# Attention stage of a two-layer encoder: where a gated eviction, the last projection units and the softmax bound stand

## The chip, the cores and the metric

One NeuronCore of one Trainium2 chip runs the whole kernel in a single launch. The metric is the device time of one execution in microseconds; the median of several runs counts. The engines are TensorE (PE, with PEld for its weight loads), VectorE (DVE), ScalarE (ACT), GpSimd (POOL) and SyncE (SP, which here only issues the weight DMAs). Each engine runs its own list of instructions in order, and they meet through semaphores.

## The reference

Two post-norm layers over x of shape (1, 512, 1024). What matters here, per layer:

```python
proj = jnp.einsum("btd,de->bte", x, w_in)            # q/k/v of the delta rule, z, beta, decay, q/k/v of attention, gates
...                                                  # branch A: gated delta rule, 8 heads of 128, both directions
o_dn = (o_dn * lax.rsqrt(jnp.mean(o_dn * o_dn, axis=-1, keepdims=True) + RMS_EPS)
        * dn_norm_w * jax.nn.silu(z))
...                                                  # branch B: attention, 16 query heads, 4 key heads, |i - j| <= 128
p = jax.nn.softmax(jnp.concatenate([s, sink], axis=-1), axis=-1)[..., :-1]
o = jnp.einsum("bnhgqk,bnkhd->bnqhgd", p, vb)
gate_a, gate_b = jnp.split(jax.nn.sigmoid(gates), 2, axis=-1)
merged = gate_a * (o_dn @ w_branch_a) + gate_b * (o_sw @ w_branch_b)
x = layer_norm(DN_ALPHA * x + merged @ w_out, ...)
x = layer_norm(DN_ALPHA * x + swiglu_ffn(x, ...), ...)
```

The softmax of a query has one extra column, the head's sink logit, in its maximum and in its denominator.

## The kernel before

**Weights.** All weights arrive as units of 128 x 1024 f32 over one queue (SP, L437) into three slots. A slot is loaded again when TensorE has finished the unit in it. POOL splits each unit into a high part (L488) and a low part (L491); TensorE forms each product as high x high, high x low and low x high (L527, L528, L529). A unit of features has 8 steps of three 512-column matmuls into one PSUM bank.

**The delta-rule stage.** 24 q/k/v units come first. Then 8 heads run one after another (levels of a triangular inverse, then a scan of 4 steps). Between their dependent matmuls TensorE does fill work, taken from a fixed list: `FILL` is the order in which the 28 units of z, gate A and attention's q, k, v are streamed, and `ORDER` adds work without weights to it: ("o", i) turns head i's normed output with 4 transposes, ("t", i) turns a value tile. `SHARE` and `SHARE_LAST` say how many steps are done at which spot of a head; what is left after the last head is done behind the scores of attention's block 0 (`fill(len(STEPS) - filled[0])`). Entries alternate between PSUM banks 6 and 7; an entry starts only when the one two before it has been evicted (`fill_free`). ACT evicts z, g, q, k, v and t in `fill_out`; DVE evicts o and multiplies it by dn_norm and silu(z) (L1549), and forms the cosine part of q and k. At the end of `ORDER` stand v0, o0, z7, t0, o1, o2, g7, o3, o4, v1, o5, o6, t1, o7. In the last head ACT also scales the outputs of the earlier heads and takes silu of their z (`head_out`).

**Attention.** 16 blocks n (4 groups of heads g x 4 blocks of 128 queries b), each against 2 or 3 key blocks. Per block: TensorE scores (L887, masks L892) into banks 0 to 2; DVE takes the row maximum (`stats`, L1666), the bound with the sinks (L1669), its negative (L1671) and the sink term (L1672); ACT forms the exponentials with their sums (L1274) and that of the sink (L1277); DVE adds to the denominator and takes the reciprocal (L1694, L1696); TensorE turns the probabilities (L929) into banks 4 to 6; ACT copies the first of them (L1288), DVE the others (L1705); TensorE multiplies by the values (L943), DVE scales (L1711). Into each block TensorE also puts one unit, half before and half behind the value matmuls: `block_unit(n)`, in bank 3, for n < 8 a gate B unit, for n >= 8 one of W_A. It starts when unit n-1 has been evicted (`att_free`), by ACT for gate B and by DVE's `branch_a` (L1684) for W_A, with its gate multiplied in. In DVE's loop over n, `branch_a(n - 9)` stands behind the denominators and behind `stats(n + 1)`, ahead of the copies of pT.

What sets all orders is the program text; there is no planner. Merging, output projection, layer norms and the feed-forward follow and are not touched.

Of the kernel before, what the change touches and what calls it, by code (L numbers as in the profile page):

```python
# [17 lines left out]
F32 = mybir.dt.float32  # L18
# [8 lines left out]
P = 128  # L27
SEQ = 512
D = 1024
DEPTH = 2  # L30
# [51 lines left out]
for _h in range(0, HEADS, 2):  # L82
    _a, _b, _c = SIDE[_h // 2 * 3:_h // 2 * 3 + 3]
    FILL += [("z", _h), ("g", _h), _a, _b, ("z", _h + 1), ("g", _h + 1), _c]


ORDER = [(kind, n, f) for f, (kind, n) in enumerate(FILL)]
_at = {(kind, n): p for p, (kind, n, f) in enumerate(ORDER)}
ORDER = (ORDER[:_at["v", 0] + 1] + [("o", 0, None), ORDER[_at["z", 7]], ("t", 0, None), ("o", 1, None), ("o", 2, None),
       ORDER[_at["g", 7]], ("o", 3, None), ("o", 4, None), ORDER[_at["v", 1]], ("o", 5, None), ("o", 6, None),  # L90
       ("t", 1, None), ("o", 7, None)])
STEPS = [(p, k) for p, (kind, n, f) in enumerate(ORDER) for k in range(1 if f is None else KT)]


# [23 lines left out]
def trunk(nc, x_in, stream, w_ba, conv_w, a_log, dt_bias, dn_norm, sinks, ln_rows, ln_cols, consts, masks, trig_in, out):  # L118
    with ExitStack() as ctx:
# [39 lines left out]
        exp_a = place("exp_a", [P, DEPTH * 16], F32)  # L159
        dtb = place("dtb", [P, DEPTH * 16], F32)  # L160
        snk = place("snk", [P, DEPTH * 16], F32)
        tab = place("tab", [P, HEADS, 6, 2, CHUNKS], F32)
        rn = place("rn", [P, 2 * HEADS, CHUNKS], F32)
        rno = place("rno", [P, HEADS, CHUNKS], F32)
# [95 lines left out]
        def flat(ap):  # L260

            return ap.rearrange("p c t -> p (c t)")
# [251 lines left out]
        def _(pe):  # L514
# [109 lines left out]
            for l in range(0, DEPTH):  # L624
# [11 lines left out]

                feature_pair(l * PAIRS + AT_QKV, l * 16)

                pe.wait_ge(ready_bf, 7)
                pe.wait_ge(ba_split, l * 2 + 2)  # L640
                for k in range(KT):
                    ins = product(PS[0:32, 4, :], bah[:, k, :], bal[:, k, :], xh[:, k, :], xl[:, k, :],
# [339 lines left out]
        def _(act):  # L982
# [49 lines left out]
            for l in range(0, DEPTH):  # L1032
# [45 lines left out]
                def head_out(i):  # L1078

                    for c in range(CHUNKS):  # L1080
                        ins = A(o_dn[:, i, c, :], o_dn[:, i, c, :], ACT.Copy, scale=rno[:, i, c:c + 1])
                    ins.then_inc(on_ready, 1)
                    z = flat(raw[:, i, :, :])
                    A(z, z, ACT.Silu).then_inc(z_silu, 1)

# [93 lines left out]
                def head(h, s, more):  # L1179
                    n = l * HEADS + h  # L1180
                    for lev in range(1, 7):
                        for r in range(2):
                            act.wait_ge(vx_mm[r], n * 6 + lev)
                            if lev in BLOCK_LEVELS:
                                new = PS[:, 3 * r + 2, :].rearrange("p (c t) -> p c t", c=CHUNKS)
                                for a, b in new_blocks(lev, r == 1):
                                    ins = copy(X[r][a, :, b], new[a, :, b])
                                ins.then_inc(x_upd[r], 1)
                            else:
                                copy(X[r][:].rearrange("p c t -> p (c t)"), PS[:, 3 * r + 2, :]).then_inc(x_upd[r], 1)  # L1190
                        if lev % 2 == 0:
                            fill_out(ISSUED[h, f"L{lev}"])
                        if not more and lev == 1:
                            act.wait_ge(rno_dve, l * 4 + 1)
                            A(rno[:, 0:HEADS - 1, :], rno[:, 0:HEADS - 1, :], ACT.Sqrt).then_inc(rno_act, 1)
                        if not more and lev > 1:
                            act.wait_ge(rno_dve, l * 4 + 2)
                            head_out(lev - 2)
                    for r in range(2):
                        act.wait_ge(e_mm[r], n + 1)  # L1200
                        A(V[r][:].rearrange("p c t -> p (c t)"), PS[:, 3 * r, :], ACT.Copy,
                          scale=E_SCALE).then_inc(e_ready[r], 1)
                    if more:
                        front_turned(n + 1, 1 - s)
                        fill_out(ISSUED[h, "E"])
                    else:
                        head_out(5)
                    for step in range(CHUNKS):
                        chunk = (step, CHUNKS - 1 - step)
                        for r in range(2):  # L1210
# [17 lines left out]
                        if step == 1:  # L1228
# [2 lines left out]
                            fill_out(ISSUED[h, "S0"])  # L1231
                            if not more:
                                head_out(6)
                        if step == 2:
                            fill_out(ISSUED[h, "S1"])
                    fill_out(ISSUED[h, "S2"])
# [15 lines left out]

                act.wait_ge(rno_dve, l * 4 + 3)
                A(rno[:, HEADS - 1, :], rno[:, HEADS - 1, :], ACT.Sqrt).then_inc(rno_act, 1)
                fill_out(ORDER.index(("o", 5, None)))
                act.wait_ge(rno_dve, l * 4 + 4)
                head_out(HEADS - 1)
                fill_out(len(ORDER))

                def group_out(g):  # L1260
# [4 lines left out]
                for n in range(GROUPS * CHUNKS):  # L1265
                    g, b = divmod(n, CHUNKS)
                    m = l * GROUPS * CHUNKS + n
                    nb = min(b + 2, CHUNKS) - max(b - 1, 0)
                    act.wait_ge(stats_step, m * 4 + 3)
                    if n > 0:  # L1270
                        act.wait_ge(p_turned, m)
                        act.wait_ge(den_step, m * 2)
                    for q in range(GQ):
                        A(pr[:, q, 0:nb, :], PS[:, 0:nb, q * P:(q + 1) * P], ACT.Exp, bias=mn[:, q:q + 1],  # L1274
                          scale=ATT_SCALE, accum_out=den[:, q:q + 1]).then_inc(probs, 1)
                    act.wait_ge(stats_step, m * 4 + 4)
                    A(es[:], es[:], ACT.Exp).then_inc(sink_exp, 1)  # L1277
                    if b == 0 and g > 0:
                        group_out(g - 1)
                    if 1 <= n <= KT:  # L1280
# [66 lines left out]
        def _(dve):  # L1347
# [17 lines left out]
            for r in range(2):  # L1365
                TS(neg_bf[r][:], tri[r], 1.0, NEG_BIG, ALU.subtract, ALU.mult).then_inc(ready_bf, 1)
            nc.vector.memset(ln_rs[:], 0.0).then_inc(ready_bf, 1)
            for s in range(2):
                dve.sem_inc(ff_h, 1)
            dve.wait_ge(ready_bf, 7)  # L1370

            def output_gain(l, n, c):
                m = l * 2 + n
# [10 lines left out]
            for l in range(0, DEPTH):  # L1384
# [267 lines left out]
                head(HEADS - 1, 1, False)  # L1652
                dve.wait_ge(o_ss, (l + 1) * HEADS)
                TS(rno[:, HEADS - 1, :], rno[:, HEADS - 1, :], 1.0 / P, RMS_EPS, ALU.mult, ALU.add).then_inc(rno_dve, 1)
                fill_out(ORDER.index(("o", 3, None)))
                dve.wait_ge(rno_act, l * 2 + 2)
                nc.vector.reciprocal(rno[:, HEADS - 1, :], rno[:, HEADS - 1, :]).then_inc(rno_dve, 1)

                def stats(n):
# [5 lines left out]
                    dve.wait_ge(scores, m + 1)  # L1665
                    nc.vector.tensor_reduce(mx[:], PS[:, 0:hi - lo, :].rearrange("p j (q t) -> p q j t", q=GQ),  # L1666
                                            mybir.AxisListType.XY, ALU.max).then_inc(stats_step, 1)
                    dve.wait_ge(stats_step, m * 4 + 1)
                    STT(mx[:], mx[:], ATT_SCALE, sinks_of, ALU.mult, ALU.max).then_inc(stats_step, 1)  # L1669
                    dve.wait_ge(stats_step, m * 4 + 2)  # L1670
                    TS(mn[:], mx[:], -1.0, None, ALU.mult).then_inc(stats_step, 1)  # L1671
                    TT(es[:], sinks_of, mx[:], ALU.subtract).then_inc(stats_step, 1)  # L1672

                def group_out(g):
                    for t, bk in ((0, 2), (1, 6)):
# [12 lines left out]
                for n in range(GROUPS * CHUNKS):  # L1688
                    g, b = divmod(n, CHUNKS)
                    m = l * GROUPS * CHUNKS + n  # L1690
                    lo, hi = max(b - 1, 0), min(b + 2, CHUNKS)
                    dve.wait_ge(probs, m * 4 + 4)
                    dve.wait_ge(sink_exp, m + 1)
                    TT(den[:], den[:], es[:], ALU.add).then_inc(den_step, 1)  # L1694
# [3 lines left out]
                        group_out(g - 1)  # L1698
                    if b > 0 and n < GROUPS * CHUNKS - 1:
                        stats(n + 1)  # L1700
                    if n > KT:
                        branch_a(n - 1 - KT)
                    dve.wait_ge(p_turned, m + 1)
                    for j in range(1, hi - lo):
                        ins = nc.vector.tensor_copy(pT[:, j, :], PS[:, 4 + j, :])  # L1705
# [231 lines left out]
```

## Time and profile before

| | us |
|---|---|
| runs, median of 3 | 2601.8 (2597.61 to 2605.43) |
| profiled execution | 2598.42 |
| its span, first to last instruction | 2596.6 |
| PE busy | 2422.8 (93%) |
| DVE busy | 1145.5 (44%) |
| POOL busy | 1134.9 (44%) |
| ACT busy | 789.1 (30%) |
| attention of layer 0, about | 600 to 820 |
| attention of layer 1, about | 1890 to 2103 |

Busy times are of instructions that compute; waits aren't in them. A wait is shown in brackets behind the instruction that ended it, with what released it. Matmuls overlap, so that a 512-column matmul shows 0.39 us while the next starts 0.23 us later.

### The profile page before, as it was taken

To read this page: it belongs to the slowest core of one execution; us is meant where nothing else is said; L and a number is where in the kernel's file an instruction comes from. 1 tells how busy PE (TensorE), PEld (TensorE's weight loads), DVE (VectorE), ACT (ScalarE), POOL (GpSimd) and SP (SyncE) were. 2 spreads that over 40 slices of the span, in tenths; PEclk is the share of its full clock that TensorE was granted. 3 is DMA by queue.
4 is the path that set the end of the run, shared out by engine and by line. 5 is a ranking of instruction groups with operands and counts; after the bars stand their busy time and mean duration, and the time that the engine had idled before them with its cause. 6 is when DMAs were issued, how large, how long until landed. Compare 5 with 4: busy or idle time off the path is not lost.

```text
span 2596.6 us, 35628 instructions
## 1 busy us (share of the span) xinstructions
PE 2422.8 (93%) x14240; PEld 1998.1 (77%) x14240; DVE 1145.5 (44%) x2066; ACT 789.1 (30%) x2114; POOL 1134.9 (44%) x674
## 2 busy tenths in 40 slices
PE   8999999988988989999999999999889898999997
PEld 6877877777877778888778778778778777788885
DVE  4666677653333251110156666766533335411103
ACT  3644433453322021110045444434543221211100
POOL 4543232323323646666545432332332246566665
PEclk9999999999999999999999999999999999999999
DMA  3221111111112323333222111111111133233332
GB/s 129 90 66 42 38 50 44 40 38 41 41 33 98 106 73 97 98 98 97 91 98 82 58 49 38 46 41 38 46 41 41 33 106 113 74 97 97 114 94 85
DMA packets 53252, 181.69 MB, mean 70 GB/s; under 512 B 7392, under 2 KB 8032, under 8 KB 53088
## 3 DMA queue, kind: packets, MB, share of 16 engines
q1 hardware_dynamic: 44496, 160.71, 20.1%
q10 hardware_dynamic: 8592, 18.69, 2.3%
q8 instruction: 114, 1.87, 0.3%
q14 instruction: 50, 0.41, 0.1%
HBM read 169.94 MB, written 4.19 MB: 67 GB/s over the span
## 4 chain that ended last, share of the span: by engine, by line
PE 76%; DVE 13%; ACT 5%; issue 3%; DMA 1%; POOL 1%; ACTq 0%; DVEq 0%; SPq 0%; POOLq 0%
PE PS L527 20%; PE PS L528 19%; PE PS L529 19%; PE PS L887 3%; DVE Y L1599 3%; PE PS L943 2%; DMA w_raw<-stream 1%; PE PS L761 1%; PE PS L848 1%; ACT DT L1144 1%; DVE att L1666 1%; PE PS L705 1%; ACT pr L1274 1%; PE PS L772 1%; DVE V L1587 1%
## 5 line engine op out<-in xcount | busy, mean ns | idle before, releaser
L488 POOL TENSOR_SCALAR wh<-w_raw 128x1024 fp32r<-128x1024 f32 (+1 forms) x301 | 323.5, 1075 | 1350.6 <-DMA w_raw<-stream 1350.2
L491 POOL TENSOR_TENSOR wl<-w_raw,wh 128x1024 fp32r<-128x1024 f32 (+1 forms) x301 | 722.6, 2401 | 25.1
L527 PE MATMUL PS<-xh,wh 128*128 128x512 f32 x1664 | 689.4, 414 | 19.6 <-POOL wl L491 6.9
L529 PE MATMUL PS<-xl,wh 128*128 128x512 f32 x1664 | 658.3, 396 | 0.0
L528 PE MATMUL PS<-xh,wl 128*128 128x512 f32 x1664 | 657.0, 395 | 0.0
L527 PEld LDWEIGHTS PS<-xh,wh 128*128 128x128 f32 x1664 | 318.7, 192 | 79.1 <-POOL wl L491 8.2
L529 PEld LDWEIGHTS PS<-xl,wh 128*128 128x128 f32 x1664 | 317.4, 191 | 69.9
L528 PEld LDWEIGHTS PS<-xh,wl 128*128 128x128 f32 x1664 | 319.5, 192 | 55.2
L1500 DVE SCALAR_TENSOR_TENSOR conv_acc<-PS,cw,conv_acc 128x510 f32<-128x510 f32 x192 | 143.9, 749 | 120.5 <-ACT conv_acc L1113 115.3
L1848 DVE TENSOR_TENSOR hf<-sg,PS 128x512 f32<-128x512 f32 x44 | 30.2, 687 | 357.7 <-PE PS L529 357.7
L527 PE MATMUL PS<-wh,hh 128*128 128x512 f32 x352 | 138.9, 395 | 3.4 <-POOL wl L491 3.4
L528 PE MATMUL PS<-wh,hl 128*128 128x512 f32 x352 | 140.3, 398 | 0.0
L529 PE MATMUL PS<-wl,hh 128*128 128x512 f32 x352 | 138.1, 392 | 0.0
L1739 DVE SCALAR_TENSOR_TENSOR x<-x,PS 128x1024 f32<-128x1024 f32 x12 | 14.6, 1220 | 279.1 <-PE PS L529 279.1
L1587 DVE TENSOR_TENSOR V<-PS,lev_mask 128x512 f16<-128x512 f32 x192 | 123.5, 685 | 12.9 <-PE PS L761 10.1
L1190 ACT CAST X<-PS 128x512 f16<-128x512 f32 x128 | 73.7, 586 | 133.4 <-PE PS L780 123.6
L1666 DVE TENSOR_REDUCE att<-PS 128x4 f32<-128x1024 f32 (+1 forms) x32 | 47.7, 1489 | 130.1 <-PE PS L892 92.8
L1335 ACT ACTIVATE hh<-hf 128x512 fp32r<-128x512 f32 x44 | 27.8, 632 | 252.5 <-DVE hf L1848 252.5
L1599 DVE TENSOR_TENSOR Y<-PS,Y 128x512 f16<-128x512 f32 x128 | 85.4, 688 | 27.3 <-PE PS L772 27.2
L1320 ACT ACTIVATE ln_rs<-ln_rs 128x1 f32<-128x1 f32 x16 | 3.2, 203 | 293.4 <-DVE ln_rs L1762 293.4
L1274 ACT ACTIVATE pr<-PS,att 128x256 f32<-128x256 f32 (+1 forms) x128 | 65.9, 529 | 82.8 <-DVE att L1671 82.8
L772 PE MATMUL PS<-V,X 128*128 128x128 f16 x768 | 75.6, 221 | 15.0 <-DVE V L1587 5.8
(249 smaller groups left out, 4084.3 us busy)
## 6 DMA issues: line engine op xcount, KB each, us to landing
w_raw<-stream SPq DMA_DIRECT2D x300, 512.0 KB, 3.5
x<-x_in ACTq DMA_DIRECT2D x6, 512.0 KB, 7.2
qx<-qx ACTq DMA_DIRECT2D x48, 64.0 KB, 2.0
raw<-raw ACTq DMA_DIRECT2D x32, 64.0 KB, 2.1
ln_g<-ln_rows ACTq DMA_DIRECT2D x4, 512.0 KB, 4.3
ln_b<-ln_rows ACTq DMA_DIRECT2D x4, 512.0 KB, 5.8
x_park<-x ACTq DMA_DIRECT2D x4, 512.0 KB, 4.9
x<-x_park ACTq DMA_DIRECT2D x4, 512.0 KB, 6.6
```

Source lines behind the costliest of these rows:

```text
L488: nc.gpsimd.tensor_scalar(wh[s][:, w], w_raw[s][:, w], 1.0, 1.0, ALU.mult, ALU.mult).then_inc(w_hi_done, 1)
L491: nc.gpsimd.tensor_tensor(wl[s][:, w], w_raw[s][:, w], wh[s][:, w].bitcast(F32), ALU.subtract).then_inc(split_done, 1)
L527: mm(o, ah, bh, start=first, stop=False)
L528: mm(o, al, bh, start=False, stop=False)
L529: return mm(o, ah, bl, start=False, stop=last)
L772: ins = mm(PS[:, 3 * r + 1, c * P:(c + 1) * P], X[r][:, c, :], V[r][:, c, :], start=True, stop=True)
L887: ins = mm(PS[:, j, q * P:(q + 1) * P], qx[:, g // 2 * GQ + q, b * P:(b + 1) * P], kz[:, g, (lo + j) * P:(lo + j + 1) * P], start=q == 0, ...
L1190: copy(X[r][:].rearrange("p c t -> p (c t)"), PS[:, 3 * r + 2, :]).then_inc(x_upd[r], 1)
L1274: A(pr[:, q, 0:nb, :], PS[:, 0:nb, q * P:(q + 1) * P], ACT.Exp, bias=mn[:, q:q + 1], scale=ATT_SCALE, accum_out=den[:, q:q + 1]).then_inc( ...
L1500: STT(conv_acc[s][:, lo:hi], PS[:, s, lo + d:hi + d], w, conv_acc[s][:, lo:hi], ALU.mult, ALU.add).then_inc(conv_step, 1)
L1587: TT(V[r][:], bank(3 * r), rows(y_mask[r][lev]), ALU.mult).then_inc(v_ready[r], 1)
L1599: TT(Y[r][:], bank(3 * r + 1), Y[r][:], ALU.add).then_inc(y_upd[r], 1)
```

## The change

In the order of units, z7 and g7 come ahead of v0 and v1, and the tail of `ORDER` is o0, v0, o1, o2, t0, o3, o4, v1, o5, o6, t1, o7. Silu of z is taken apart from `head_out` (`z_out`), so that the last head's has been taken before the end of the scan. ACT's exponentials become a function, and those of block 0 are called ahead of the last evictions of the fill list; two intermediate `fill_out` calls (one on ACT, one on DVE) fall away. On DVE the bound is formed by one operation from the row maximum and a stored negative of the sinks, and `branch_a` moves to the front of its block.

```diff
+FILL[-7:] = [("z", 6), ("g", 6), ("q", 7), ("z", 7), ("g", 7), ("v", 0), ("v", 1)]
...
-ORDER = (ORDER[:_at["v", 0] + 1] + [("o", 0, None), ORDER[_at["z", 7]], ("t", 0, None), ("o", 1, None), ("o", 2, None),
-       ORDER[_at["g", 7]], ("o", 3, None), ("o", 4, None), ORDER[_at["v", 1]], ("o", 5, None), ("o", 6, None),
-       ("t", 1, None), ("o", 7, None)])
+ORDER = (ORDER[:_at["v", 0]] + [("o", 0, None), ORDER[_at["v", 0]], ("o", 1, None), ("o", 2, None), ("t", 0, None),
+       ("o", 3, None), ("o", 4, None), ORDER[_at["v", 1]], ("o", 5, None), ("o", 6, None), ("t", 1, None), ("o", 7, None)])
...
+                def z_out(i):
+                    at = ORDER.index(("z", i, FILL.index(("z", i))))
+                    act.wait_ge(fill_free[at % 2], released(l, at) + 1)
                     z = flat(raw[:, i, :, :])
                     A(z, z, ACT.Silu).then_inc(z_silu, 1)
...
                             head_out(lev - 2)
+                            z_out(lev - 2)
...
                         head_out(5)
+                        for i in (5, 6):
+                            z_out(i)
...
                                 head_out(6)
+                                z_out(7)
...
-                fill_out(ORDER.index(("o", 5, None)))
-                act.wait_ge(rno_dve, l * 4 + 4)
-                head_out(HEADS - 1)
-                fill_out(len(ORDER))
...
+                def probabilities(n):
...
+                    act.wait_ge(stats_step, m * 3 + 2)
                     if n > 0:
                         act.wait_ge(p_turned, m)
                         act.wait_ge(den_step, m * 2)
                     for q in range(GQ):
                         A(pr[:, q, 0:nb, :], PS[:, 0:nb, q * P:(q + 1) * P], ACT.Exp, bias=mn[:, q:q + 1],
                           scale=ATT_SCALE, accum_out=den[:, q:q + 1]).then_inc(probs, 1)
+                    act.wait_ge(stats_step, m * 3 + 3)
                     A(es[:], es[:], ACT.Exp).then_inc(sink_exp, 1)
+
+                act.wait_ge(rno_dve, l * 4 + 4)
+                head_out(HEADS - 1)
+                probabilities(0)
+                fill_out(len(ORDER))
...
+            TS(neg_snk[:], snk[:], -1.0, None, ALU.mult).then_inc(ready_bf, 1)
...
-                fill_out(ORDER.index(("o", 3, None)))
                 dve.wait_ge(rno_act, l * 2 + 2)
...
-                    STT(mx[:], mx[:], ATT_SCALE, sinks_of, ALU.mult, ALU.max).then_inc(stats_step, 1)
-                    dve.wait_ge(stats_step, m * 4 + 2)
-                    TS(mn[:], mx[:], -1.0, None, ALU.mult).then_inc(stats_step, 1)
-                    TT(es[:], sinks_of, mx[:], ALU.subtract).then_inc(stats_step, 1)
+                    STT(mn[:], mx[:], -ATT_SCALE, neg_snk[:, l * 16 + g * GQ:l * 16 + (g + 1) * GQ], ALU.mult,
+                        ALU.min).then_inc(stats_step, 1)
+                    dve.wait_ge(stats_step, m * 3 + 2)
+                    TT(es[:], sinks_of, mn[:], ALU.add).then_inc(stats_step, 1)
...
+                    if n > KT:
+                        branch_a(n - 1 - KT)
                     dve.wait_ge(probs, m * 4 + 4)
...
                     if b > 0 and n < GROUPS * CHUNKS - 1:
                         stats(n + 1)
-                    if n > KT:
-                        branch_a(n - 1 - KT)
```

## Rows read from the trace of the kernel before

**Rows 1.** The page: busy time, chain by engine, a group (busy us, mean ns).
```profile
PE 2422.8 (93%) x14240; PEld 1998.1 (77%) x14240; DVE 1145.5 (44%) x2066; ACT 789.1 (30%) x2114; POOL 1134.9 (44%) x674
...
PE 76%; DVE 13%; ACT 5%; issue 3%; DMA 1%; POOL 1%; ACTq 0%; DVEq 0%; SPq 0%; POOLq 0%
...
L1190 ACT CAST X<-PS 128x512 f16<-128x512 f32 x128 | 73.7, 586 | 133.4 <-PE PS L780 123.6
```

**Rows 2.** TensorE's waits, layer 0: engine line <- releaser: total us, times, longest.
```profile
PE PS L527 <- DVE raw L1684: 13.2, 6, 4.5
```

**Rows 3.** TensorE's waits in the attention of layer 1.
```profile
PE PS L527 <- DVE raw L1684: 11.3, 6, 3.5
```

**Rows 4.** Timeline, block 9, layer 0: start, duration, instruction [idle before <- releaser].
```profile
724.92 1.47 PE L929 MATMUL PS<-cst,pr 128*128 128x128 f32 x12
...
726.46 2.34 POOL L491 TENSOR_TENSOR wl<-w_raw,wh 128x1024 fp32r<-128x1024 f32 x1
726.92 1.90 DVE L1669 SCALAR_TENSOR_TENSOR att<-att,snk 128x4 f32<-128x4 f32 x1
...
729.00 0.68 DVE L1684 TENSOR_TENSOR raw<-raw,PS 128x512 f32<-128x512 f32 x1
...
729.60 1.28 DVE L1705 COPY pT<-PS 128x512 f32<-128x512 f32 x2
...
729.83 0.76 PE L527 MATMUL PS<-ozh,wh 128*128 128x512 f32 x1 [3.43 <-DVE raw L1684]
...
734.10 1.11 PE L943 MATMUL PS<-v_tok,pT 128*128 128x64 f32 x9
```

**Rows 5.** Timeline: first half of the unit in block 10, layer 0.
```profile
744.21 0.47 PE L527 MATMUL PS<-ozh,wh 128*128 128x512 f32 x1 [1.16 <-DVE raw L1684]
...
747.09 2.79 PE L943 MATMUL PS<-v_tok,pT 128*128 128x64 f32 x24
```

**Rows 6.** Timeline of block 5, layer 0.
```profile
672.80 0.17 DVE L1671 TENSOR_SCALAR att<-att 128x4 f32<-128x4 f32 x1
672.84 2.37 POOL L491 TENSOR_TENSOR wl<-w_raw,wh 128x1024 fp32r<-128x1024 f32 x1
672.88 2.35 DVE L1672 TENSOR_TENSOR att<-snk,att 128x4 f32<-128x4 f32 x1
...
676.53 3.75 PE L943 MATMUL PS<-v_tok,pT 128*128 128x64 f32 x24 [2.51 <-issue]
```

**Rows 7.** Timeline: scores behind a group's first block, layer 0.
```profile
615.03 1.13 PE L887 MATMUL PS<-kz,qx 128*128 128x128 f32 x8 [0.22 <-ACT pr L1274]
```

**Rows 8.** Timeline: last scan of layer 0, and from it to block 0's probabilities.
```profile
571.73 0.66 PE L673 MATMUL PS<-cst,o_dn 128*128 128x128 f32 x4 [2.23 <-ACTq L1059]
...
583.54 0.18 DVE L1657 RECIPROCAL rno<-rno 128x4 f32<-128x4 f32 x1 [1.35 <-ACT rno L1254]
...
586.82 0.75 DVE L1549 SCALAR_TENSOR_TENSOR raw<-PS,dn_w,raw 128x512 f32<-128x512 f32 x1 [0.21 <-PE PS L673]
...
593.20 1.28 ACT L1081 ACTIVATE o_dn<-o_dn,rno 128x128 f32<-128x128 f32 x4
...
600.52 1.94 PE L929 MATMUL PS<-cst,pr 128*128 128x128 f32 x8 [5.10 <-ACT pr L1274]
```

**Rows 9.** Chain that ended last, 560 to 625: start, us on it, what.
```profile
573.48 0.85 PE PS L848 x4
...
594.49 1.28 ACT L1084
...
598.29 1.95 ACT pr L1274 x8
```

**Rows 10.** Windows behind block 0's wait, both layers: busy by engine, PEclk, DMA, GB/s.
```profile
600.50:607.00 6.50, 6.48 (x20) 5.47 (x21) 0.95 (x3) 1.43 (x3) 2.51 (x2) 0.53 0.01 3
...
1889.00:1896.00 7.00, 5.36 (x24) 4.79 (x25) 1.03 (x3) 3.05 (x10) 3.24 (x3) 0.76 0.01 2
```

More of the change, by code:

```diff
@@ L161, in trunk @@
         snk = place("snk", [P, DEPTH * 16], F32)
+        neg_snk = place("neg_snk", [P, DEPTH * 16], F32)
         tab = place("tab", [P, HEADS, 6, 2, CHUNKS], F32)
@@ L637, in _ @@
                 feature_pair(l * PAIRS + AT_QKV, l * 16)
-                pe.wait_ge(ready_bf, 7)
+                pe.wait_ge(ready_bf, 8)
                 pe.wait_ge(ba_split, l * 2 + 2)
@@ L1254, in _ @@
                 A(rno[:, HEADS - 1, :], rno[:, HEADS - 1, :], ACT.Sqrt).then_inc(rno_act, 1)
-                fill_out(ORDER.index(("o", 5, None)))
+                def probabilities(n):
+                    g, b = divmod(n, CHUNKS)
+                    m = l * GROUPS * CHUNKS + n
+                    nb = min(b + 2, CHUNKS) - max(b - 1, 0)
+                    act.wait_ge(stats_step, m * 3 + 2)
+                    if n > 0:
+                        act.wait_ge(p_turned, m)
+                        act.wait_ge(den_step, m * 2)
+                    for q in range(GQ):
+                        A(pr[:, q, 0:nb, :], PS[:, 0:nb, q * P:(q + 1) * P], ACT.Exp, bias=mn[:, q:q + 1],
+                          scale=ATT_SCALE, accum_out=den[:, q:q + 1]).then_inc(probs, 1)
+                    act.wait_ge(stats_step, m * 3 + 3)
+                    A(es[:], es[:], ACT.Exp).then_inc(sink_exp, 1)
                 act.wait_ge(rno_dve, l * 4 + 4)
                 head_out(HEADS - 1)
+                probabilities(0)
                 fill_out(len(ORDER))
@@ L1267, in _ @@
                     m = l * GROUPS * CHUNKS + n
-                    nb = min(b + 2, CHUNKS) - max(b - 1, 0)
-                    act.wait_ge(stats_step, m * 4 + 3)
                     if n > 0:
[L1271 to L1277, printed above, removed]
+                        probabilities(n)
                     if b == 0 and g > 0:
@@ L1367, in _ @@
             nc.vector.memset(ln_rs[:], 0.0).then_inc(ready_bf, 1)
+            TS(neg_snk[:], snk[:], -1.0, None, ALU.mult).then_inc(ready_bf, 1)
             for s in range(2):
                 dve.sem_inc(ff_h, 1)
-            dve.wait_ge(ready_bf, 7)
+            dve.wait_ge(ready_bf, 8)
             def output_gain(l, n, c):
@@ L1667, in stats @@
                                             mybir.AxisListType.XY, ALU.max).then_inc(stats_step, 1)
-                    dve.wait_ge(stats_step, m * 4 + 1)
-                    STT(mx[:], mx[:], ATT_SCALE, sinks_of, ALU.mult, ALU.max).then_inc(stats_step, 1)
-                    dve.wait_ge(stats_step, m * 4 + 2)
-                    TS(mn[:], mx[:], -1.0, None, ALU.mult).then_inc(stats_step, 1)
-                    TT(es[:], sinks_of, mx[:], ALU.subtract).then_inc(stats_step, 1)
+                    dve.wait_ge(stats_step, m * 3 + 1)
+                    STT(mn[:], mx[:], -ATT_SCALE, neg_snk[:, l * 16 + g * GQ:l * 16 + (g + 1) * GQ], ALU.mult,
+                        ALU.min).then_inc(stats_step, 1)
+                    dve.wait_ge(stats_step, m * 3 + 2)
+                    TT(es[:], sinks_of, mn[:], ALU.add).then_inc(stats_step, 1)
                 def group_out(g):
```

## The prediction, made before the changed kernel was seen or timed

> **What bounds the kernel now.** I read the page first: TensorE is busy for 93% of the span and carries 76% of the chain that ended last, with DVE 13% and ACT 5% behind it [rows 1]. So a change pays only where TensorE stands still or runs at its lower clock. I then listed TensorE's waits in the two attention stretches, which are what the diff touches. The largest entry is matmuls of a unit that wait for `branch_a` (L1684): 13.2 us in 6 waits in layer 0, and 11.3 us in 6 waits in layer 1 [rows 2, 3]. Next comes the first transpose of block 0's probabilities, which waits 5.10 us for the exponentials [rows 8]. The timeline shows why the first wait exists. In block 9, DVE goes through the row maximum, the bound and the sink term before it evicts the W_A unit; the unit's bank is free only at 729.7, so TensorE, done with its transposes at 726.4, stands for 3.43 us [rows 4]. The window after block 0's wait is granted 0.53, about the 1.2 GHz level [rows 10]: a long wait is paid twice.
>
> **Part 1: the gated eviction ahead of the denominators.** `branch_a(n-9)` needs the unit of block n-1, which TensorE finishes just before it scores block n+1, and a gate that is ready since block 7. Placed first, it runs in 0.68 us [rows 4] beside the scoring matmuls. Queued behind it on DVE stand the denominators and the next row maximum; the maximum waits for scores that come 2 to 3 us later (the reduction of block 10 could not start before TensorE had gone through all three key blocks), so 0.68 us is hidden. If that cover were gone it would cost 7 x 0.68 = 4.8 us per layer. The removed waits sum to 13.2 + 11.3 = 24.5 us.
> Two corrections. The clock: in block 9 of layer 0 the four product steps from 729.83 to 734.10 take 4.27 us, against 2.88 us from 744.21 to 747.09, where the wait was only 1.16 [rows 4, 5]. That is 1.4 us lost to the lower clock. Block 9 of layer 1, whose wait is nearly the same (3.5, the longest there), and block 13 of layer 0, with the longest wait of all (4.5), get the same 1.4 as an estimate. Together +4.2. What is late next: the pV matmuls (L943) wait for the DVE copies of pT. In block 9 the bound L1669 takes 1.90 us instead of its usual 0.16 and ends with GpSimd's wl subtraction (726.46 + 2.34). Without the eviction between, the two copies (1.28) end near 730.3, while TensorE gets there at 726.2 + 2.8 = 729.0. So some 1.4 us of the 3.43 come back, 1.3 in layer 1's block 9 and about 2 in block 13 of layer 0: -4.7. In the eight short waits (1.2 to 1.6 us) the copies are done over 1 us before TensorE asks. Part 1 gives 24.5 + 4.2 - 4.7 = 24.0 us; bounds 18 (every block gives back 0.5 us more) and 29 (no giving back).
>
> **Part 2: the bound in one step.** STT with negated factors, min for max, and the stored -sinks makes `mn` directly; the TENSOR_SCALAR L1671 (0.17 us, 0.20 from start to start) goes, and ACT's exponentials start 0.2 us earlier. TensorE feels it only where block 1 of a group follows: there it waits 0.2 to 0.3 us for the exponentials [rows 7]. 8 such blocks x 0.2 = 1.6 us. In the other 24 blocks it is hidden by the product steps. The added start-up negation, one DVE operation on 32 columns, lies beside the first projection units: 0.
> The missing operation also moves the sink term up by 0.08 us. In block 5 of layer 0 that matters: L1671 ran at 672.80, GpSimd's wl took over at 672.84, and the sink term L1672 then took 2.35 us; the pV matmuls waited 2.51 us and 24 of them took 3.75 us [rows 6] instead of about 2.7. If L1672 starts at 672.80 it slips through, which is worth 2.1 + 1.0 + about 1.5 for the product steps behind, some 4.5 us; block 13 of layer 0 has the same pattern, worth 2. The bounds are 0 (it is caught just the same) and 6.5. I take 3, near the middle, since 0.04 us decides it.
> A rule of the Trainium skill bears on this (SBUF — State Buffer, "Who interferes with whom"): DVE operations with two SBUF inputs share a read port with GpSimd, and whichever was issued first holds it for its whole length. Rows 6 agree, with 2.35 us. By the rule the sink term would slip through in both places, and this part would give 8 us in place of 4.6. By the same rule the new STT and the sink term stay as exposed as before.
>
> **Part 3: z7 and g7 ahead of v0, v1.** The same 234 steps, rearranged; weights come in the new order through the same three slots, each unit at most two steps earlier, and the split was waiting for freed slots all along. In the last head's scan the step-2 spot was o1/o2 behind the copy of a turned value tile: 2.23 us of wait [rows 8], and then scan matmuls at 0.85 us for 4 [rows 9], which at the higher clock would be half of that, 0.4 less in each of three groups. In the new order this spot is two steps of v0. Against it, v0's first step waits for ACT's copy of g7 in the step before (about 1.3 us, where 0.8 is waited now), and two more product steps (0.7 each, from 2.88 / 4) go into the scan for two groups of transposes (at most 0.66 each) that leave it. I get the end of the scan 2.4 us earlier.
> The tail is a swap. ACT no longer evicts v0 before the first exponentials: `probabilities(0)` stands ahead of the last `fill_out`. TensorE scores block 0, does the last step of v0 and o1 (to about 581.1), and then o2 waits for v0's bank. ACT: reciprocal now ends at 583.7, so 581.3; head scaling 1.28; table load 1.28; exponentials 1.95; copy 0.6, as other copies of 512 columns take on ACT [rows 1]: 586.4 [rows 8, 9]. That is 5.3 us of idle, in place of the 5.10 at 600.52. One silu and one table load less stand in this chain (1.9 us): they moved to places in the scan where ACT idles. From 586.4 on: o2, t0, o3, o4 with waits for each other's evictions (0.75 each on DVE), 3.0 us; eight steps of v1, 5.5; o5, o6, t1, o7 and the last eviction, 3.9. The probabilities are turned at 598.8, 1.7 earlier than 600.52. The clock: the old idle was followed by 6.5 us at 0.53 in layer 0 (3.0 us lost) and 7 us at 0.76 in layer 1 (1.7 lost) [rows 10]. The new one is followed by a stretch that is half waits; I put its loss at 1 to 2.3 us. Net: 1.7 + 3.0 - (1 to 2.3) in layer 0, 1.7 + 1.7 - (1 to 2.3) in layer 1, in sum 3.5 to 6.1. I take 4.5, toward the lower half, because the waits inside may draw the low clock out. Bounds: -5 (the eight steps of v1 at half clock too) and +8 (clock never falls).
>
> **Sum.** 24.0 + 1.6 + 3 + 4.5 = 33.1 us. The profiled execution took 2598.4 (span 2596.6), so 2565.3; the median of the runs shown, 2601.8, is 3.4 above it. On that footing: 2569.
>
> **Rivals.**
> (a) The eviction's wait passes to the copies of pT. For: it already happens in blocks 1, 5, 9 and 13. Against: in the short-wait blocks there is 1 us of slack. If GpSimd's split lands 1 us earlier relative to the scores, all eight short waits come back at about 1 us, and nothing slips through: 33 - 8 - 3 = 22 us, 2580.
> (b) The tail costs instead of giving: o2's idle of 5.3 us leaves TensorE at the lower clock through v1, or ACT's queue (v0, then t0) holds each bank longer. Part 3 becomes -5: 33 - 9.5 = 23.5, 2578. For: five short waits follow the long one. Against: eight product steps without a break are in there.
> (c) Slower. DVE's small operations between SBUF tiles meet GpSimd's subtraction in more blocks than now, since the period of a block changes and the phase of split and scores with it. One meeting costs 2.2 to 2.5 us of wait and up to 2 of clock [rows 6], say 4. It is met in about 7 of 32 blocks now; it takes 9 more meetings to undo the 33 us, 12 make it 2614. For: the split starts 3.7 to 5 us after a unit's end, close to the bound. Against: in blocks with two key blocks the bound is made 0.4 us before the split starts, and the removed wait doesn't stand between them.
> (d) The change doesn't do what it says: the unit behind `branch_a` isn't complete when DVE reaches it, DVE stands, and TensorE's wait keeps 80%. Gain 9 or 10: 2592. Nothing in the trace speaks for it, since TensorE runs in that order.
>
> **How the numbers follow.** Forecast 0.60 (own range 2561 to 2575), (a) 0.15, (b) 0.16, (c) 0.04, (d) 0.05. The range for 8 in 10: low end all bounds on the good side but one (40 us), high end just past (a) and (b): 2560 to 2583. A difference under 0.3% (7.8 us) can't be told from none here. Faster takes forecast, (a), (b) and most of (d): 0.94; same 0.03; slower 0.03.
>
> **What would show it.** In the waits of TensorE, the entry for L1684 falls from 24.5 us to under 2, and L943's grows by 3 to 5; in block 9 L1684 starts within 1 us of the unit's end. L1671's TENSOR_SCALAR is gone, and ACT starts exponentials 0.2 us after the bound's start. In the tail the 5.1 us wait of L929 disappears and one near 5.3 us appears at L673 (o2) behind ACT's exponentials; in the scan the 2.23 us wait is gone. The forecast is wrong if L943 waits over 1 us in most blocks from 9 on, if the tail from the scan's end to the first L929 grows longer than the 20 us of now, or if DVE is seen standing before L1684 with the maximum behind it.

## The result, and the profile after

The changed kernel takes 2563.3 us (median of 4 runs, 2559.85 to 2565.64), the kernel before 2601.5; the ratio is 0.9854, 95% interval 0.9834 to 0.9874. That is 38 us less where the prediction had 33, and inside its range. The profiled execution took 2559.85, its span 2557.9.

The page of the changed kernel, busy times and chain by engine, to be held against [rows 1]:

```profile
PE 2411.8 (94%) x14240; PEld 1992.5 (78%) x14240; DVE 1139.2 (45%) x2035; ACT 785.6 (31%) x2112; POOL 1134.8 (44%) x674
...
PE 79%; DVE 11%; ACT 4%; issue 3%; DMA 1%; POOL 1%; ACTq 0%; DVEq 0%; SPq 0%; POOLq 0%
```

TensorE's work is the same 14240 matmuls, but it shows 11 us less busy, since fewer of them ran at the lower clock (its mean granted clock is 0.985 of full speed, 0.981 before); the other 27.7 us of the span's 38.7 are idle time that went. DVE issues 31 instructions less: 32 small operations went, one came in at the start. ACT issues two less, the two table loads. TensorE's waits in the attention of layer 0, then of layer 1:

```profile
PE PS L944 <- issue: 3.8, 2, 2.5
PE PS L528 <- DVE swl L1696: 1.6, 1, 1.6
PE PS L930 <- ACT pr L1275: 1.4, 1, 1.4
PE PS L930 <- DVEq L1569: 1.0, 1, 1.0
```

```profile
PE PS L944 <- issue: 5.2, 3, 2.4
```

The gated eviction (L1684 before, L1701 now), which led this list with 24.5 us [rows 2, 3], is gone from it. What stands first now are the value matmuls (L944). Block 9 of layer 0, the one of [rows 4], shows both; columns are start, duration, instruction and the wait in front:

```profile
716.47 0.69 DVE L1701 TENSOR_TENSOR raw<-raw,PS 128x512 f32<-128x512 f32 x1 [2.16 <-PE PS L530]
717.07 0.16 DVE L1713 TENSOR_TENSOR att<-att,att 128x4 f32<-128x4 f32 x1
...
719.49 1.47 PE L930 MATMUL PS<-cst,pr 128*128 128x128 f32 x12
...
720.72 0.48 PE L528 MATMUL PS<-ozh,wh 128*128 128x512 f32 x1
...
721.18 2.40 POOL L492 TENSOR_TENSOR wl<-w_raw,wh 128x1024 fp32r<-128x1024 f32 x1
721.48 2.12 DVE L1686 SCALAR_TENSOR_TENSOR att<-att,neg_snk 128x4 f32<-128x4 f32 x1
...
723.71 1.28 DVE L1722 COPY pT<-PS 128x512 f32<-128x512 f32 x2
725.10 1.64 PE L944 MATMUL PS<-v_tok,pT 128*128 128x64 f32 x13 [1.35 <-issue]
```

The eviction starts 3 us before the transposes do, so the unit starts at 720.72 without a wait. The bound on DVE is still held until GpSimd's subtraction ends at 723.58, the copies of pT queue behind it, and 1.35 us come back at the value matmuls: the forecast had 1.4.

The tail of layer 0 in the changed kernel, against [rows 8, 9]:

```profile
583.44 1.28 ACT L1082 ACTIVATE o_dn<-o_dn,rno 128x128 f32<-128x128 f32 x4 [0.24 <-DVE rno L1674]
...
584.74 1.28 ACT L1275 ACT_TABLE_LOAD   x1
...
586.03 0.47 ACT L1275 ACTIVATE pr<-PS,att 128x256 f32<-128x256 f32 x1
...
587.94 0.59 ACT L1068 COPY raw<-PS 128x512 f32<-128x512 f32 x1
...
588.63 1.12 PE L674 MATMUL PS<-cst,o_dn 128*128 128x128 f32 x4 [5.20 <-ACTq L1071]
...
602.36 1.06 PE L930 MATMUL PS<-cst,pr 128*128 128x128 f32 x8 [0.99 <-DVEq L1569]
```

The 5.10 us in front of block 0's transposes have turned into 5.20 us in front of o2, behind v0's copy, as forecast.

To compare stretches I take start times of the same work from the timelines (us, layer 0 / layer 1). The scan is that of the last head and starts with its first L836, L837 now. Score n stands for the scoring matmuls of block n, and the tail is the stretch from score 0 to block 0's transposes. What a block takes is the interval from the start of the scaling of the block before to the start of its own, so there are fifteen intervals behind block 0.

| stretch | before | after |
|---|---|---|
| start of the scan to score 0 | 19.66 / 19.61 | 17.03 / 17.04 |
| score 0 to block 0's transposes | 20.14 / 20.13 | 22.29 / 22.30 |
| those to score 1 | 6.50 / 4.98 | 3.67 / 3.66 |
| start of the scan to block 0's scaling (o_g) | 51.75 / 50.17 | 48.37 / 48.38 |
| from it to block 15's scaling | 204.17 / 198.20 | 183.76 / 183.78 |

Layer 0 and 1 of the kernel before ran the same instructions, 6 us apart; after the change the sums agree, but by chance: block 5 took 12.90 and 14.16 us, block 8 16.27 and 14.73.

### The profile page after: what moved, and what is told of

It is laid out like the page before. It is cut to its first block, busy times and chain, and to the rows that moved or that the text cites. A ratio compares the mean times of both kernels' runs of the same rounds, so it can differ in the third digit from the quotient of the medians.

```text
span 2557.9 us, 35595 instructions
## 1 busy us (share of the span) xinstructions
PE 2411.8 (94%) x14240; PEld 1992.5 (78%) x14240; DVE 1139.2 (45%) x2035; ACT 785.6 (31%) x2112; POOL 1134.8 (44%) x674
## 4 chain that ended last, share of the span: by engine, by line
PE 79%; DVE 11%; ACT 4%; issue 3%; DMA 1%; POOL 1%; ACTq 0%; DVEq 0%; SPq 0%; POOLq 0%
PE PS L528 20%; PE PS L530 20%; PE PS L529 20%; DVE Y L1617 3%; PE PS L888 3%; PE PS L944 3%; PE PS L930 1%; DMA w_raw<-stream 1%; PE PS L762 1%; PE PS L849 1%; ACT DT L1149 1%; PE PS L706 1%; PE PS L773 1%; DVE V L1605 1%; PE PS L837 1%
## 5 line engine op out<-in xcount | busy, mean ns | idle before, releaser
L1617 DVE TENSOR_TENSOR Y<-PS,Y 128x512 f16<-128x512 f32 x128 | 85.5, 689 | 27.0 <-PE PS L773 26.9
```

The lines of the kernel that those rows point to most:

```text
L1617: TT(Y[r][:], bank(3 * r + 1), Y[r][:], ALU.add).then_inc(y_upd[r], 1)
```

## The experiments

Times are medians, ratios are to the kernel before, run on the same chip with the kernel in question; its median there was 2604.4 in the first four runs and 2604.0 in the last four.

**e1_gated**, the kernel before with one part:

```diff
+                    if n > KT:
+                        branch_a(n - 1 - KT)
                     dve.wait_ge(probs, m * 4 + 4)
...
-                    if n > KT:
-                        branch_a(n - 1 - KT)
                     dve.wait_ge(p_turned, m + 1)
```

> The kernel before with one part of the change: the gated eviction of a W_A unit stands first in its block, ahead of the denominators. Theory: the six waits per layer for it go, TensorE's own loss is each wait plus 0.25 us for restarting plus the lower clock behind it, and some 1.4 us come back at the value matmuls of block 9: 13 to 15 us less in layer 0 and 11 to 13 in layer 1, 24 to 28 in sum, about 2575. Rival, the wait passes on to the copies of pT in most blocks: 12 to 15 us, about 2588. Rival, this part carries all of the measured 38 us: about 2563.

2584.8 us, ratio 0.9919 (0.9892 to 0.9947), so 21 us less, 14 to 28 by the interval. 24 to 28 were expected; the interval reaches both that and the rival's 12 to 15. The rival's mechanism, a wait passed on in most blocks, did not show: it was passed on in blocks 9 and 13 alone. The eviction is gone from the waits, but those at the value matmuls are 6.8 us in 4 waits in layer 0 and 8.1 in 4 in layer 1. Block 13 of layer 0 shows why:

```profile
776.73 1.05 POOL L488 TENSOR_SCALAR wh<-w_raw 128x1024 fp32r<-128x1024 f32 x1 [9.95 <-DMA w_raw<-stream]
...
777.26 0.52 DVE L1669 SCALAR_TENSOR_TENSOR att<-att,snk 128x4 f32<-128x4 f32 x1
...
777.82 0.17 DVE L1671 TENSOR_SCALAR att<-att 128x4 f32<-128x4 f32 x1
777.86 2.38 POOL L491 TENSOR_TENSOR wl<-w_raw,wh 128x1024 fp32r<-128x1024 f32 x1
777.90 2.37 DVE L1672 TENSOR_TENSOR att<-snk,att 128x4 f32<-128x4 f32 x1
...
780.19 1.28 DVE L1705 COPY pT<-PS 128x512 f32<-128x512 f32 x2
781.56 5.08 PE L943 MATMUL PS<-v_tok,pT 128*128 128x64 f32 x24 [2.02 <-issue]
```

The bound ends with GpSimd's first operation (777.78), L1671 takes the short opening, and L1672 is held by the second. TensorE waits 2.02 us, and its 24 value matmuls then take 5.08 us for the usual 2.8, at a granted clock of 0.53. So the eviction's wait was in block 13 partly a cover over another one.

**e2_bound**, the kernel before with the bound in one step:

```diff
-                    STT(mx[:], mx[:], ATT_SCALE, sinks_of, ALU.mult, ALU.max).then_inc(stats_step, 1)
-                    dve.wait_ge(stats_step, m * 4 + 2)
-                    TS(mn[:], mx[:], -1.0, None, ALU.mult).then_inc(stats_step, 1)
-                    TT(es[:], sinks_of, mx[:], ALU.subtract).then_inc(stats_step, 1)
+                    STT(mn[:], mx[:], -ATT_SCALE, neg_snk[:, l * 16 + g * GQ:l * 16 + (g + 1) * GQ], ALU.mult,
+                        ALU.min).then_inc(stats_step, 1)
+                    dve.wait_ge(stats_step, m * 3 + 2)
+                    TT(es[:], sinks_of, mn[:], ALU.add).then_inc(stats_step, 1)
```

> The kernel before with one part of the change: the bound of the exponentials in one step. Theory of the forecast: 0.2 us in each of eight blocks, and in blocks 5 and 13 of layer 0 the sink term slips in front of GpSimd's subtraction: 3 to 8 us less, 2594 to 2599. Rival, the missing operation matters nowhere because TensorE has its product steps to do: within 1 us of before. Rival, it is the phase between weight arrival and scores that decides which blocks are caught, not this operation: blocks 5 and 13 are caught just the same or others are, any sum from -5 to +5.

2592.2 us, ratio 0.9953 (0.9934 to 0.9972), 12 us less, 7 to 17 by the interval, where 3 to 8 were expected: one small operation of 0.17 us, taken out 32 times. Block 5 of layer 0, to be held against [rows 6]:

```profile
673.51 1.05 POOL L489 TENSOR_SCALAR wh<-w_raw 128x1024 fp32r<-128x1024 f32 x1 [10.60 <-DMA w_raw<-stream]
673.63 0.94 DVE L1671 SCALAR_TENSOR_TENSOR att<-att,neg_snk 128x4 f32<-128x4 f32 x1
674.61 0.16 DVE L1674 TENSOR_TENSOR att<-snk,att 128x4 f32<-128x4 f32 x1
...
674.65 2.37 POOL L492 TENSOR_TENSOR wl<-w_raw,wh 128x1024 fp32r<-128x1024 f32 x1
674.69 1.28 DVE L1707 COPY pT<-PS 128x512 f32<-128x512 f32 x2
676.07 2.86 PE L944 MATMUL PS<-v_tok,pT 128*128 128x64 f32 x24 [0.20 <-issue]
```

GpSimd leaves 0.09 us between its two operations. The sink term now takes the opening that L1671 had: it starts 0.04 us ahead of the subtraction and takes 0.16 us, and the copies follow. The wait of 2.51 us is 0.20. This was so in blocks 5 and 13 of both layers, so the second rival, that it is left to the phase, did not hold there; in block 1 the bound itself was held, in both layers.

**e3_tail**, the changed kernel with the bound in two steps and `branch_a` behind `stats` again, so that the order of the fill list, `z_out` and block 0's exponentials ahead of the last evictions alone remain:

```diff
-                    if n > KT:
-                        branch_a(n - 1 - KT)
                     dve.wait_ge(probs, m * 4 + 4)
...
+                    if n > KT:
+                        branch_a(n - 1 - KT)
                     dve.wait_ge(p_turned, m + 1)
```

> The kernel before with one part of the change: the order of the last fill entries, silu of z apart, and block 0's exponentials ahead of the last evictions. Theory: from the scan of the last head to the first value matmul 3.4 us less in layer 0 and 1.8 in layer 1, as in the changed kernel, about 2596.5. Rival, the tail gives nothing by itself and what was seen comes from a shorter bound: within 1 us of before. Rival, it costs 1.6 us in the last head's levels in both layers: about 2600.

2600.3 us, ratio 0.9990 (0.9976 to 1.0003): by time alone it can't be told from no change. By the stretches of the table it can: scan 17.06 and 17.05, tail 23.15 and 22.27, then 3.67 twice, to block 0's scaling 49.33 and 48.44 against 51.75 and 50.17. That is 2.4 and 1.7 us less, where 3.4 and 1.8 were expected. The levels ahead of the scan take 15.0 us in layer 1, from the last head's wait for ACT's X on, where the kernel before, e1 and e2 have 14.7; in layer 0 they take 14.7 to 16.4 us in kernels of either order.

**e4_pt_first**, the changed kernel with the copies of pT first:

```diff
-                    if b > 0 and n < GROUPS * CHUNKS - 1:
-                        stats(n + 1)
                     dve.wait_ge(p_turned, m + 1)
...
                     ins.then_inc(pT_dve, 1)
-                    if b == 0:
+                    if n < GROUPS * CHUNKS - 1:
                         stats(n + 1)
```

> The changed kernel with DVE's copies of pT ahead of the next block's maximum in every block, not in a group's first alone. Theory: the five waits left at the value matmuls (2.46, 1.35, 2.42, 1.36, 1.39 us, in blocks 1, 5 and 9) come from small DVE operations that are held while GpSimd subtracts, and matter only because the copies queue behind them; with the copies in front all five go, with their restart and the lower clock behind two of them: 9 to 14 us less than the changed kernel, 2550 to 2554. Rival, the later maximum makes the exponentials late, since they now start 1.3 us later: waits for them appear at the next block, and the time is that of the changed kernel or above.

2546.3 us, ratio 0.9780 (0.9753 to 0.9808). By the ratios that is 19 us below the changed kernel, by the fifteen intervals of the profiled executions 15.5; 9 to 14 were expected. Block 9 of layer 0:

```profile
714.42 1.29 DVE L1720 COPY pT<-PS 128x512 f32<-128x512 f32 x2 [3.56 <-PE PS L930]
714.52 2.40 POOL L492 TENSOR_TENSOR wl<-w_raw,wh 128x1024 fp32r<-128x1024 f32 x1
715.62 1.75 DVE L1683 TENSOR_REDUCE att<-PS 128x4 f32<-128x1536 f32 x1
717.02 2.79 PE L944 MATMUL PS<-v_tok,pT 128*128 128x64 f32 x24
```

No value matmul waits any more, though DVE's bound and sink term are still held for 1.2 to 2.4 us, 17 times in the two layers. The copies and the maximum, which read PSUM, run beside the subtraction at their usual length. Blocks 1, 5, 9 and 13 take 12.6 us each in both layers, and the fifteen intervals 176.0 us. The exponentials are later, but no wait for them has grown (1.44 us in block 8, 1.43 in the changed kernel), so the rival fell.

**e5_v0_first**, the changed kernel with one line more on ACT:

```diff
+                fill_out(ORDER.index(("o", 1, None)))
                 act.wait_ge(rno_dve, l * 4 + 4)
                 head_out(HEADS - 1)
                 probabilities(0)
```

> The changed kernel with ACT's eviction of v0 put back in front of the last head's scaling and block 0's exponentials. Theory: the 5.2 us wait at o2 was that eviction behind the exponentials; now o2, t0 and o3 run in the gap and the wait moves to o4, which needs t0's copy, still behind the exponentials, and is 2 us shorter: 2 to 3 us less per layer, 4 to 6 less than the changed kernel, ratio to before about 0.983. Rival, the wait at o2 is for something else (the reciprocal, the scores): no change. Rival, the tail is bound by the eight steps of v1 behind the exponentials, so that moving transposes gives nothing: within 1 us.

2561.6 us, ratio 0.9833 (0.9817 to 0.9850); the tail is 21.3 and 21.5 us instead of 22.3. The wait is for the eviction, as the first theory says; it broke into three (1.3 at t0, 0.3 at o3, 1.5 at o4), but only 0.9 us per layer came out, where 2 to 3 were expected: three groups of transposes are all the work that this moves, and each waits for an eviction of the one two before. The ratio came out at the 0.983 expected, but it can't bear the theory: its interval overlaps that of the changed kernel, and the profiled execution was no shorter (2559.7 us of span against 2557.9).

**e6_v1_gap**, e5 with the eight steps of v1 put in the gap:

```diff
-ORDER = (ORDER[:_at["v", 0]] + [("o", 0, None), ORDER[_at["v", 0]], ("o", 1, None), ("o", 2, None), ("t", 0, None),
-       ("o", 3, None), ("o", 4, None), ORDER[_at["v", 1]], ("o", 5, None), ("o", 6, None), ("t", 1, None), ("o", 7, None)])
+ORDER = (ORDER[:_at["v", 0]] + [("o", 0, None), ORDER[_at["v", 0]], ("o", 1, None), ORDER[_at["v", 1]], ("o", 2, None),
+       ("o", 3, None), ("t", 0, None), ("o", 4, None), ("o", 5, None), ("t", 1, None), ("o", 6, None), ("o", 7, None)])
```

> As e5_v0_first, and the eight steps of v1 come right behind o1, so that they run while ACT makes block 0's exponentials. Theory: the wait of 5.2 us and the lower clock behind it go, the last evictions follow one another with 0.2 to 0.4 us waits: the tail from score 0 to the first turned probabilities falls from 22.3 us to 15 or 16, 12 to 14 us less than the changed kernel, ratio to before 0.979 to 0.981. Rival, the chain of evictions (eight on DVE at 0.75, three on ACT) binds instead: the tail stays over 19 us, 6 us less.

2554.6 us, ratio 0.9809 (0.9794 to 0.9824). The tail is 16.9 us in both layers, 5.4 less; 15 or 16 were expected, and the ratio is inside the range given for it. 3 us of the 10.8 were given back in blocks 1 (17.61 and 16.94 us, where the changed kernel has 15.78 and 15.70):

```profile
612.31 2.04 DVE L1687 SCALAR_TENSOR_TENSOR att<-att,neg_snk 128x4 f32<-128x4 f32 x1
614.28 2.48 POOL L503 TENSOR_TENSOR ozl<-raw,ozh 128x512 fp32r<-128x512 f32 x2
614.38 1.18 DVE L1690 TENSOR_TENSOR att<-snk,att 128x4 f32<-128x4 f32 x1
...
616.87 5.35 PE L944 MATMUL PS<-v_tok,pT 128*128 128x64 f32 x24 [2.33 <-issue]
```

The wait there was in the changed kernel too; this time the lower clock held for all 24 matmuls (granted 0.50).

**e7_split_late**, the changed kernel with GpSimd's split moved away from DVE's small operations, and nothing else:

```diff
+                    k = u % UNITS - U_QKV - U_FILL
+                    if 2 <= k < U_ATT:
+                        pool.wait_ge(pT_dve, l * GROUPS * CHUNKS + k - 1)
                     pool.wait_ge(loaded[s], u // SLOTS * 16 + 16)
```

> The changed kernel in which GpSimd splits attention's units from the third on only after DVE's copies of pT of the block; nothing moves on DVE. Theory: the waits left at the value matmuls come from small DVE operations held by GpSimd's subtraction; with the subtraction moved away, blocks 5, 9 and 13 take 12.6 us each without any wait, as in e4_pt_first, and only block 1, whose unit is not delayed, keeps its wait: 4 to 7 us less than the changed kernel. Rival, the operations are slow by themselves or by the maximum before them: they stay at 1 to 2 us, and the time is that of the changed kernel. Rival, the later split makes TensorE wait for weights: slower.

2546.4 us, ratio 0.9780 (0.9766 to 0.9795), the same as e4 by another road. Block 9 of layer 0:

```profile
715.93 0.16 DVE L1689 SCALAR_TENSOR_TENSOR att<-att,neg_snk 128x4 f32<-128x4 f32 x1
716.13 0.16 DVE L1692 TENSOR_TENSOR att<-snk,att 128x4 f32<-128x4 f32 x1
716.21 1.28 DVE L1725 COPY pT<-PS 128x512 f32<-128x512 f32 x2
717.71 1.04 POOL L492 TENSOR_SCALAR wh<-w_raw 128x1024 fp32r<-128x1024 f32 x1 [14.57 <-DVE pT L1725]
718.04 2.79 PE L947 MATMUL PS<-v_tok,pT 128*128 128x64 f32 x24
```

With the subtraction gone from under them, the bound takes 0.16 us (2.12 before) and the sink term 0.16; the fifteen intervals are 177.5 and 176.0 us. The 17 us gained are far more than the 4 to 7 expected. My expectation erred on block 1: its unit is delayed too, and it took 12.6 us like the others, 3.1 to 3.2 less in each layer. The long durations are therefore not the operations' own, and no wait for the later split appears.

**e8_combo**, e4 and e6 together.

> e4_pt_first and e6_v1_gap together. Theory: the two gains lie in different stretches and add: 12 to 14 us below e4_pt_first, about 2532, ratio to before 0.972 to 0.974. Rival, they share the lower clock behind block 0 and give less: 2538. Rival, the value matmuls of block 0 now come before v_tok or pT is ready: 2542 or more.

2536.6 us (2535.6 to 2537.3), ratio 0.9742 (0.9727 to 0.9756): the fastest, 67 us below the kernel before and by the ratios some 29 below the changed one. It came 4.6 us above the 2532 that I had expected, nearer to the rival's 2538, and not for the rival's reason: the tail kept its 16.9 us in both layers with a granted clock of 1.00. In its profile the sums are 42.95 + 175.98 and 42.98 + 177.56 us for the two layers, against 48.43 + 176.07 and 48.45 + 176.03 in e4: 9.5 us less, not the 12 to 14 that I had taken over from e6's expectation, in which I had put the tail at 15 to 16. 1.5 us of the difference lie in block 8 of layer 1, which met the lower clock here and not in e4.

## Why the prediction was right, and where its terms were off

**Direction and size.** 33 us forecast, 38 measured (33 to 43 by the interval). To size the parts, take the fifteen intervals behind block 0. With the old order on DVE and the old bound (the kernel before and e3) they took 204.2, 198.2, 201.4 and 204.2 us, mean 202.0; with the eviction first alone 194.2 and 195.5; with the new bound alone 195.9 and 197.7; with both (the changed kernel and e5) 183.8, 183.8, 183.2 and 184.2. These are single executions. The last column has what the medians of all runs give, halved for one layer, with the interval.

| per layer | forecast | by intervals | by the runs |
|---|---|---|---|
| part 1 alone | 12.0 | 7.2 | 10.5 (6.9 to 14.1) |
| part 2 alone | 2.3 | 5.2 | 6.1 (3.6 to 8.6) |
| both | 14.3 | 18.3 | not run |
| part 3 | 2.3 | 2.3 (2.6 from the scan on, less 0.3 in the levels); 1.8 in e3 | 1.3 (-0.4 to 3.1), e3 |
| all | 16.6 | 20.6 | 19.0 (16.4 to 21.6) |

By the intervals that is 41 us in sum, where the profiled executions differ by 38.6. That the sum came out near is in part luck: part 2 gave more than twice its term, and part 1 rather less than its own (clearly by the intervals, within the noise by the runs).

**Part 1: mechanism right, size too large.** The six waits per layer went, and block 9 gave back 1.35 us. By the intervals part 1 alone gave 14.4 us in both layers, below its lower bound of 18; by the runs 21, inside the bounds. The four short waits per layer gave 1.4, 1.8, 1.7 and 1.4 us in layer 0 (blocks 10, 11, 12, 14) where the trace had called them 1.16, 1.59, 1.37 and 1.16: each costs 0.25 us more than its row says. The row counts from the recorded end of the transposes, but without a wait the unit starts 0.24 us ahead of that end (720.72 against 719.49 + 1.47 in block 9 above). It is no restart of TensorE, as I had it in the expectation of e1: the first matmul shows 0.47 us behind the wait [rows 5] and 0.48 without one. The forecast left this out, 2 us in sum. It was also wrong to book all of block 13 here. Its wait in layer 0 stood behind the held sink term as well as behind the order on DVE:

```profile
784.90 2.32 DVE L1672 TENSOR_TENSOR att<-snk,att 128x4 f32<-128x4 f32 x1
787.14 0.67 DVE L1684 TENSOR_TENSOR raw<-raw,PS 128x512 f32<-128x512 f32 x1
787.96 0.77 PE L527 MATMUL PS<-ozh,wh 128*128 128x512 f32 x1 [4.48 <-DVE raw L1684]
```

With the eviction first alone (e1) 2.02 and 2.48 us of wait are left in block 13 of the two layers, at the value matmuls; with the new bound alone (e2) 2.14 and 2.15, at the unit; with both none.

**Part 2: the term that was mis-sized.** The term is "I take 3, near the middle, since 0.04 us decides it". The sink term slips through where the bound ends with GpSimd's first operation, and the new bound made that the same in both layers: blocks 5 and 13 took 13.0 and 15.0 us in both layers of e2, where the old bound had 14.1 to 16.4 and 15.5 to 18.9. That is what the prediction had drawn from the rule it cites, by which this part would have been 8 us; e2 gave 10.4 by the intervals and 12 by the runs. I had looked at layer 0 only for the pattern; e3, with the same code, was caught in block 13 of both layers (18.7 and 18.9). The other term of part 2, 0.2 us in each of eight blocks, came to nothing where it can be read. The wait for the exponentials stood only in blocks 1 and 5 of each layer (0.21 to 0.22 us) and is gone in e2, but in block 1 the one at the value matmuls grew by as much or a little more: 2.20 to 2.38 and 2.24 to 2.48.

**Do the parts add?** By the runs they do within the noise: 21 + 12 + 3 = 36 us for the three singly, 38 for all. By the intervals 5.9 of the 18.3 us per layer are left over, but much of that is the clock of single executions: e1's profiled one was granted 0.978 in the mean, the one of the kernel before 0.981, and block 8, which no part touches, makes up 0.8 of it. What can be shown is blocks 13 and 14: 31.0 us before (mean of four), 30.0 with part 1, 27.9 with part 2, 24.3 with both, where 26.9 would be the sum. The waits of block 13 nearly add; what doesn't is the lower clock, which followed the waits of over 4 us there and in e1 also those of 2.02 and 2.48, but not the 2.1 of e2.

**Part 3: the waits right, the tail longer.** The scan gave 2.6 us (2.4 forecast). o2 waited 5.20 (5.3). From the scan's start to the turning of block 0's probabilities took 39.3 us, 0.5 less than before and not 1.7, because the clock fell behind the new wait (0.62 in the first window below, then 1.00) and the evictions of transposed outputs cost 0.3 to 1.0 us each. The tail itself grew from 20.1 to 22.3 us, one of the signs that I had named for a wrong forecast. In return the stretch to score 1 came down from 6.50 and 4.98 to 3.67 and 3.66, so that the term of 4.5 us was met: 5.2 from the scan to block 0's scaling, less 0.6 in the levels. The level stretch of the last head lost 0.3 us, which I had called free.

```profile
588.00:592.50 4.50, 3.57 (x16) 2.93 (x16) 1.45 (x2) 1.12 (x3) 2.34 (x1) 0.62 0.00 0
592.50:602.30 9.80, 8.10 (x40) 6.18 (x40) 3.06 (x5) 2.31 (x4) 0.26 (x1) 1.00 0.17 54
```

**The rivals.** (a) came true in a small part: 9.0 us of waits at the value matmuls were left, in blocks 1, 5 and 9, and e4 and e7 each took them all away. The kernel before had 8.1 us of them already, in blocks 1 and 5; they grew by 0.9 and not by the 3 to 5 that I had named as a sign, since the ones passed on in block 9 (1.35 and 1.39) were nearly offset in block 5 of layer 0 (2.51), and block 13 gave nothing back. (b) fell: the four groups of transposes behind the long wait ran at the lower clock, but v1's eight steps did not. (c) is a mechanism that decides between executions: in the kernel before, blocks 5, 6 and 13 took 7.8 us more in layer 0 than in layer 1, where the waits of 5 and 13 were 1.13 and 2.55 us in place of 2.51 and 4.48. But it worked for the change. Its 2614 was counted from the profiled execution; on the footing of the others it is 2617. (d) did not occur: DVE waited 2.16 us for the unit with nothing due behind it.

**What stays open.** Why the same wait is sometimes followed by the lower clock and sometimes not was not tried; it moves single executions by some microseconds. Block 8, with the same wait of 1.42 to 1.44 us in front of its transposes each time, took 14.7 to 14.8 or 16.3 to 16.4 us throughout this study; in the changed kernel 704 to 708 us was granted 0.57 in layer 0, and the same place of layer 1 1.00. Parts 1 and 2 together without part 3 were not run.

## What to carry to other kernels

Before a wait is removed, ask what else would hold the same instruction a microsecond later; in block 13 a wait of 4.5 us fell to 2.0 to 2.5 with either part alone and went only with both. Size the parts of a change from several runs: intervals of single executions put part 1 at 14 us, the medians at 21. A small vector operation between a long GpSimd operation and a copy that TensorE waits for is worth more than its duration: order what TensorE needs first (e4), or order the two engines apart (e7). When a scalar engine's table load and exponentials open a gap, put matmuls with no dependence on it there, not transposes that wait for evictions (e6 against e5).

## What was not expected of the hardware

- A DVE operation on 128x4 elements with both inputs in SBUF, 0.16 us by itself, that was issued while GpSimd's 128x1024 subtraction ran ended with it, within 0.03 us in most cases, and so took up to 2.4 us; copies and maxima that read PSUM kept their length (1.29 us for two copies, 1.75 for a maximum) under the same subtraction (e4). The Trainium skill says that a DVE instruction with two SBUF inputs contends with a GpSimd instruction that reads SBUF (SBUF — State Buffer, "Who interferes with whom"), and e7 agrees: 2.12 us fell to 0.16 when the subtraction was moved.
- It isn't only the subtraction and only two inputs: the bound was also held under GpSimd's first operation (0.94 us in e2's block 5, 0.52 in e1's block 13), and L1671, with one input, took 1.20 us under a GpSimd subtraction in block 1 of both layers of the kernel before, 0.17 elsewhere. The reciprocal (0.18) kept its length.
- The opening of 0.08 us between two GpSimd operations is enough for one such operation, and the one that gets it decides 2.4 us of wait (e1 and e2, blocks 13 and 5).
- A wait of TensorE in front of a unit costs about 0.25 us over its recorded length even where the clock stays up, because work that doesn't wait starts 0.24 us ahead of the recorded end of the transposes before it. Waits of 2.0 to 2.5 us were followed by 24 value matmuls in 3.75 us [rows 6], 5.08 (e1) or 5.35 (e6) instead of 2.79, with 0.73, 0.53 and 0.50 of the clock granted.
